# A transformer block pair on one core: seven places for experts' weights and joined 4 MB transfers

## The reference, cut to what matters

```
logits = hf @ w_router + b_router;  top_vals, top_idx = top_k(logits, 4);  top_w = softmax(top_vals)
for every expert e, for the tokens that chose it (xb):
    gu = xb @ w_gate_up[e] + b_gate_up[e]             # 1024 x 2048: gate 1024 columns, up 1024 columns
    g, u = min(gu[:, :1024], 7), clip(gu[:, 1024:], -7, 7)
    y = ((u + 1) * g * sigmoid(1.702 * g)) @ w_down[e] + b_down[e]       # 1024 x 1024
x += the sum over a token's four experts of top_w * y
```

## Time and profile before

| | |
|---|---|
| three runs | 1762.68, 1765.52, 1767.84 us; median 1765.52 |
| span of the profiled execution, first to last instruction | 1762.7 us; its time with what lies around the span isn't recorded apart, the lowest of the three runs is 1762.68 |
| busy, of the span | TensorE 93%, its weight loads 59%, VectorE 40%, ScalarE 32%, GpSimd 1% |
| read from HBM | 544 MB, mean 309 GB/s |
| experts' transfers | 126 + 63 of 2048 KB into the ring, 17.4 and 16.2 us from issue to landing (medians), and a few in pieces |

### The profile page before, as it was taken

The page is one execution under the profiler, slowest core; times in us unless marked ns, Lnnn a source line. Parts: engine busy times, 40 slices in busy tenths (PEclk is TensorE's granted clock), DMA queues, the critical chain, the costliest instruction groups (busy, mean ns, idle before and its releaser), DMA issues.

```text
span 1762.7 us, 20269 instructions
## 1 busy us (share of the span) xinstructions
PE 1643.2 (93%) x8853; PEld 1036.4 (59%) x8854; DVE 707.4 (40%) x876; ACT 571.9 (32%) x787; POOL 22.5 (1%) x37
## 2 busy tenths in 40 slices
PE   8999999898889999998888888999999999999998
PEld 7788533333235454442323232378888998988886
DVE  5897411111121211211111111167664965567663
ACT  6576200011111111100000011175563765456552
POOL 0000000000000000000000000010000000000000
PEclk9999999999999999999999999999999999999999
DMA  7538999999999999999999999955555523445552
GB/s 257 174 103 289 366 392 428 427 428 427 428 427 400 428 427 425 428 427 428 428 428 428 428 427 426 420 189 193 190 192 173 184 96 120 168 132 191 191 191 96
DMA packets 118762, 546.39 MB, mean 310 GB/s; under 512 B 5696, under 2 KB 64192, under 8 KB 92976
## 3 DMA queue, kind: packets, MB, share of 16 engines
q1 hardware_dynamic: 117344, 540.96, 77.4%
q0 software_dynamic: 1040, 4.00, 0.8%
q10 hardware_dynamic: 288, 0.11, 0.0%
HBM read 544.00 MB, written 1.05 MB: 309 GB/s over the span
## 4 chain that ended last, share of the span: by engine, by line
PE 70%; DMA 25%; DVE 3%; ACT 1%; issue 1%; SPq 0%; ACTq 0%
DMA ring<-in_w_down 25%; PE PS L949 10%; PE PS L908 9%; PE PS L578 8%; PE PS L1099 6%; PE PS L580 4%; PE PS L530 2%; PE PS L531 2%; PE PS L532 2%; PE PS L850 2%; PE PS L960 2%; PE PS L563 1%; PE PS L564 1%; PE PS L565 1%; PE PS L1114 1%; PE PS L549 1%
## 5 line engine op out<-in xcount | busy, mean ns | idle before, releaser
L908 PE MATMUL PS<-ring,work 128*64 128x512 f32 x2016 | 448.2, 596 | 36.5 <-DMA ring<-in_w_gate_up 36.4
L1920 DVE TENSOR_TENSOR ring<-ring,ring 128x2048 fp32r<-128x2048 f32 (+2 forms) x130 | 289.3, 2234 | 258.5 <-ACT ring L1341 258.4
L908 PEld LDWEIGHTS PS<-ring,work 128*64 128x64 f32 x2016 | 139.7, 137 | 325.4 <-issue 246.6
L1341 ACT CAST ring<-ring 128x2048 fp32r<-128x2048 f32 (+2 forms) x131 | 242.9, 1866 | 208.8 <-DMA ring<-in_mem_w_kv 86.6
L949 PE MATMUL PS<-ring,work 128*64 128x512 f32 x1024 | 239.1, 611 | 53.8 <-DMA ring<-in_w_down 37.8
L949 PEld LDWEIGHTS PS<-ring,work 128*64 128x64 f32 x1024 | 75.4, 139 | 203.5 <-issue 164.6
L2349 DVE TENSOR_SCALAR work<-PS 128x512 f32<-128x512 f32 x32 | 22.1, 690 | 325.9 <-PE PS L908 325.9
L1596 ACT ACTIVATE work<-work 128x512 f32<-128x512 f32 x32 | 20.2, 630 | 366.2 <-DVE work L2349 366.2
L2248 DVE TENSOR_TENSOR work<-PS,work 128x512 fp32r<-128x512 f32 x32 | 22.1, 692 | 252.2 <-ACT work L1540 252.2
L578 PE MATMUL PS<-xr,ring 128*128 128x512 f32 x320 | 111.2, 392 | 0.0
L578 PE MATMUL PS<-work,ring 128*128 128x512 f32 x320 | 111.2, 392 | 0.0
(11 more groups left out here) (418 smaller groups left out, 2325.1 us busy)
## 6 DMA issues: line engine op xcount, KB each, us to landing
ring<-in_w_gate_up SPq DMA_DIRECT2D x126, 2048.0 KB, 17.4
ring<-in_w_down SPq DMA_DIRECT2D x63, 2048.0 KB, 16.2
ring<-in_ffn_w_gu SPq DMA_DIRECT2D x44, 1024.0 KB, 5.1
ring<-in_w_in SPq DMA_DIRECT2D x28, 1024.0 KB, 5.4
ring<-in_ffn_w_down SPq DMA_DIRECT2D x22, 1024.0 KB, 4.9
ring<-in_w_out SPq DMA_DIRECT2D x8, 1024.0 KB, 5.6
ring<-in_mem_w_kv SPq DMA_DIRECT2D x8, 1024.0 KB, 13.8
ring<-in_w_ple_gate SPq DMA_DIRECT2D x4, 1024.0 KB, 11.6
```

Of the source, the lines that this page charges most:

```text
L908: t = e.matmul(PS[hf * 64:hf * 64 + 64, bank, :], XG[g % 2][:, 2 * kp + kk, i * 64:(i + 1) * 64], raw_chunk(w, kk)[:, c0 + hf * 512:c0 + h ...
L1341: e.copy(hi(j), raw(j)).then_inc(*act.now(("hi", j)))
L1920: e.tensor_tensor(lo(j), raw(j), hi(j).bitcast(F32), ALU.subtract).then_inc(*dve.now(("lo", j)))
```

## The change

The list of parts stays. There are two more places: X, which is the tile `xr` made a sixth place of the ring's tensor (usable once the attention's last product is done, given up at the ple stage), and Y in work space, up to expert `CHECK`, now 6. `place` hands out the place whose part is oldest. Of experts 4 to 29 two neighbouring parts of a matrix go into two neighbouring places by one transfer of 4 MB, if the two oldest places are neighbours; it waits for both. What a partition receives is now the rows of one run of 32 KB, so a single part is half such a run. The two halves of an expert's width are therefore no longer columns 0 to 511 and 512 to 1023: `hidden` takes fours alternately, and the moving operand of gate, up and bias has four floats, then a gap of four. `apart` is issued second. To free the work space, the transposed memory `mT` is spread over leftover places, the masks `C_HM` (512 KB) come in at the end of the memory's products and not at the start, and the normed tokens for the slow path are made only in the slow path.

```diff
-CHECK = 5
+X, Y, APART = NS, NS + 1, NS + 2
+CHECK = 6
+JOINED, FIRST_JOINED = ('w_gate_up', 'w_down'), 4
+    def joined(self, i):
+        p = self.parts[i]
+        if p.name not in JOINED or not FIRST_JOINED <= p.expert < NE - 2:
+            return False
+        return (p.k0 // p.k) % 2 == 0
     def place(self):
+        first, crowded, behind = (self.of[k][0] for k in (("gate_up", 0), ("gate_up", CHECK), ("ple_gate", 0)))
+        count = dict.fromkeys(range(APART + 1), 0)
+        held = {s: s - NS for s in range(NS)}
+        i = 0
+        while i < len(self.parts):
+            if i == first:
+                held[X], held[Y] = self.of["out", 1][1] - 0.5, self.of["out", 1][1] + 0.5
+            if i == crowded:
+                del held[Y]
+            if i == behind:
+                del held[X]
+            oldest = sorted(held, key=held.get)
+            slots = oldest[:1]
+            if i == self.apart:
+                slots = [APART]
+            elif self.joined(i) and max(oldest[:2]) <= X and abs(oldest[0] - oldest[1]) == 1:
+                slots = sorted(oldest[:2])
+            after = [held[s] for s in slots if held.get(s, -1) >= 0]
...
+        early = next(n for n in self.loads if n[0] == self.apart)
+        self.loads.remove(early)
+        self.loads.insert(1 + [n[0] for n in self.loads].index(first), early)
...
+            def hidden(v, hf):
+                return v.rearrange("p (q z r) -> p q z r", z=2, r=4)[:, :, hf, :]
...
-                                             raw_chunk(w, kk)[:, c0 + hf * 512:c0 + hf * 512 + 512], start=False,
+                                             hidden(raw_chunk(w, kk)[:, c0:c0 + DE], hf), start=False,
...
-            e.wait_ge(*dve["factor_out"])
-            for h in range(2):
-                t = e.matmul(RSB[:, h * 128:(h + 1) * 128], rn[:, h:h + 1].to_broadcast([128, 128]), ident, start=True,
-                             stop=True, skip_group_check=True)
-            t.then_inc(*pe.now("rsb"))
...
-            e.dma_start(cst[:, C_HM:C_N], d["cst"][:, C_HM:C_N]).then_inc(hm_in, 16)
...
-                if g == 1:
-                    e.wait_ge(*pe["comb", 0])
+                if g == 5:
+                    e.wait_ge(*pe["beside", MEM_KV[-1]])
                     e.dma_start(p_raw, d["p"].rearrange("(h p) n -> p h n", p=128)).then_inc(p_in, 16)
+                    e.dma_start(cst[:, C_HM:C_N], d["cst"][:, C_HM:C_N]).then_inc(hm_in, 16)
...
+                    for k in after:
+                        e.wait_ge(*pe["w", k if k in plan.slot else of["out", 1][1]])
...
                     if j == plan.apart:
                         e.wait_ge(*pe["merged_t", 3])
-                        e.wait_ge(*act["bias_2", 64])
...
+                    elif n == 2:
+                        s = plan.slot[j]
+                        e.dma_start(ring_t[:, s * SLOT:(s + 2) * SLOT].rearrange("p (k n) -> p k n", n=p.n),
+                                    src).then_inc(in_memory(j)[0], 16)
                     else:
+                        if plan.slot[j] == Y:
+                            e.wait_ge(*pe["logits"])
+                            e.wait_ge(*act["bias_2", 64])
```

More of the change, by code:

```diff
@@ L163, in place @@
[L163 to L169, removed]
+        self.slot, self.at, self.loads = {}, {}, []
@@ new lines, in place @@
+        count = dict.fromkeys(range(APART + 1), 0)
[15 more added lines that the diff above has]
+            after = [held[s] for s in slots if held.get(s, -1) >= 0]
+            count[slots[0]] += 32 if i == self.apart else 16
+            for k, s in enumerate(slots):
+                self.slot[i + k], self.at[i + k] = s, (slots[0], count[slots[0]])
+                if s != APART:
+                    held[s] = i + k
+            self.loads.append((i, len(slots), after))
+            i += len(slots)
@@ L289, in stats, with in_memory @@
             return stat[:, o:o + n]
-        loaded = [sem(f"ring{i}_loaded") for i in range(NS)] + [sem("spare_loaded"), sem("apart_loaded")]
+        loaded = [sem(f"ring{i}_loaded") for i in range(NS)] + [sem(f"{n}_loaded") for n in ("place_x", "place_y", "apart")]
+        def in_memory(i):
+            return loaded[plan.at[i][0]], plan.at[i][1]
         def held(t, i, o):
@@ L1007, in crowded @@
                 with e.If(most > CAP):
+                    for c in range(8):
+                        for h in range(2):
+                            o = PS[:, 4 + c // 2, (c % 2) * 256 + h * 128:(c % 2) * 256 + h * 128 + 128]
+                            for half in (hnh, hnl):
+                                m = e.matmul(o, half[:, h, c * 128:(c + 1) * 128].bitcast(F32), ident, start=half is hnh,
+                                             stop=half is hnl, skip_group_check=True)
+                    m.then_inc(o_turned, 1)
+                    e.wait_ge(o_normed, 1)
                     with e.Fori(0, NE) as n:
@@ L2763, in sync, with load_before @@
             made = [0]
-            def load_to(i):
-                while made[0] <= i:
-                    j, p = made[0], parts[made[0]]
+            def load_before(i):
+                while made[0] < len(plan.loads) and plan.loads[made[0]][0] < i:
+                    j, n, after = plan.loads[made[0]]
                     made[0] += 1
-                    w = d[p.name]
-                    if plan.after[j] is not None:
-                        e.wait_ge(*pe["w", plan.after[j]])
+                    p, w = parts[j], d[parts[j].name]
+                    for k in after:
+                        e.wait_ge(*pe["w", k if k in plan.slot else of["out", 1][1]])
                     if p.name in PACKED:
@@ L2819, in sync @@
                         spilled(n)
-            load_to(len(parts) - 1)
+            load_before(len(parts))
             for h in range(2):
```

73 lines of the change are left out of this document (43 added, 30 removed).

## The result

| | before | after |
|---|---|---|
| median, range | 1766.68 us (1762.68 to 1768.15, 4 runs) | 1789.6 us (1788.03 to 1790.55, 4 runs) |
| ratio, 95% interval | | 1.0135 (1.0121 to 1.0149) |
| span of the profiled execution | 1762.7 us | 1788.7 us |

The forecast said slower, 1772 us with a range to 1785. The sign and the places of the loss were right; the loss of 22.9 us is nearly four times the +6.0 us of the sum, and outside the range.

The account below looks back on a forecast made before the run. The prediction took the DMA engines as the bound from 262 us to the experts' end. From 1765.5 us, -8.8 + 1.2 - 4.6 - 2.8 + 12 + 8.5 + 0.5 = +6.0 gave 1771.5, said as 1772; range 1751 to 1785.

Parts of the forecast that it names:

- The five experts whose pair starves the queue: Second gate/up pair of experts 13, 15, 16, 17, 19: DMA queue idle 2.4 us each, 12 us added.
- The places' gain: Terms for places, masks and the stretch at 524 us: -8.8 + 1.2 - 2.8 us.
- The term of the mem_w_kv stretch: Experts that also load mem_w_kv: 12 us of idle queue and 8.5 us of slower clock, +20.5 us.
- the queue holds 9.8 us: When the down pair lands in the mem_w_kv stretch, one whole pair, 9.8 us of transfer, still stands behind it.
- 2.7 us on top: Same stretch: issue to landing of an idle queue is at least 7.6 us for 4.93 us of bytes.
- The clock's 8.5: First down part before each of the five gaps slowed 1.7 us by a lower TensorE clock, 8.5 us in all.
- About 0.5 us: Crowded check at expert 6: next pair's bytes come at 28.6 us, queue lasts 28.4; bounds 0 to 2.3.
- Two more places: Start of the expert loads, 158 to 262 us: places X and Y and early apart gain 2.8 + 6.0 = 8.8 us.
- A: Rival: the queue starves in the mem_w_kv experts but the clock holds, 1763 us; chance 0.22.
- B: Rival: the queue never starves, loads behind a mem_w_kv part being issued in time, 1750.5 us; chance 0.20.
- C: Rival: the gate/up matmuls' strided moving operand costs a third, 4.6 us per expert, 1797 us; chance 0.07.
- D: Rival: the 4 MB transfer moves its bytes no faster, so no 4.6 us gain, 1776 us; chance 0.13.

Follow-up runs that it names:

- e7: Changed kernel with no joined transfers and the earlier weight layout and gathers, keeping the seven places, early apart and moved masks: 1755.55 us.
- e4: Changed kernel with three pairs of matmuls whose result nothing reads added ahead of the down parts of the mem_w_kv experts: 1786.09 us.
- e5: Changed kernel with the first joined expert 8 instead of 4: 1785.51 us.
- e10: Changed kernel, all pairs kept, with normalised rows written in the gathers' order so their stationary operand is in one piece: 1787.47 us.
- e8: Changed kernel with the mem_w_kv product ahead of the down parts and pairs only for experts 8 to 26: 1754.71 us.
- e1: Changed kernel with every 4 MB transfer taken back to two of 2 MB: 1760.8 us.
- e12: Changed kernel with every 4 MB transfer taken back to two of 2 MB, the same kernel as e1 run again: 1759.4 us.
- e9: The kernel of e8 with normalised rows written in the gathers' order so their stationary operand is in one piece: 1754.72 us.

## Why the prediction was wrong

**Right.** The bound (DMA from 262 us to the end of the experts), and so the rule that idle DMA time moves the end. The five experts whose pair starves the queue, all five. The fall of the clock after gaps of 4 us. The places' gain: e7 gave 1755.55 against 1755.1 from those terms, with some luck, since the trace has 11.7 us at the end of the experts and 10.5 at the end of the span, against 10.4. The hole at 530 closed. The moving operand by fours cost nothing: 32 gate/up matmuls in 7.03 us, 64 in 13.90, as in the earlier trace rows. The rate rose by 0.7% (427 to 428 without pairs, 430 to 431 with them in plain experts; forecast 0.65%).

The Trainium skill (DMA: Bandwidth & Descriptors, Rules for kernel authors) has 1 MiB per transfer for the maximum bandwidth; the trace differs by those 0.7%, and 431 is still short of that page's ceiling of 435.2 GB/s.

**Wrong, in order of size.**

1. The term of the mem_w_kv stretch, +20.5, measured +28.3. The failing step is "the queue holds 9.8 us" at the landing: it held 7.4 to 7.8 in four of the five cases, since TensorE waits for the last of the 16 DMA engines and most of them are 2.0 us into the next transfer by then; in the fifth, where they ended together, it held 9.1. The prediction had folded this with the start-up into "2.7 us on top", against 1.2 + 2.0 = 3.2 us at 658.70. The five holes without the clock are 14.6 us where it had 12, so this step is worth 2.6 us. The clock's 8.5 was right as a sum (8.1), in part by luck: four slow down parts of 1.4 to 2.7 us and not five of 1.7. A sixth hole of 2.1 us, at expert 13's down pair, was not forecast: I followed each hole as if the one before had not happened. It stands in every kernel that has expert 13's first hole (after, e4, e5, e10) and in none without, but that the first makes the second is my reading. The remaining 3.5 us of the lag are in no hole as counted here; that they lie beside the holes, where the rate falls before all engines stop (from 16 busy engines to none between 666.2 and 668.4) and rises again by steps, is likely and not shown.
2. "About 0.5 us" for the crowded check: 4.9. The same early end of most engines (T + 27.6, where the prediction had 28.4), and a chain to the next issue of 30.2 us instead of 26.9, in which only 0.9 us is due to the gathers. The bounds 0 to 2.3 rested on "the 1 us by which a landing trails its bytes".
3. "Two more places" with "6.0 us" from 190 to 262: the lead with the masks was 3.9 instead of 7.6. The working was right for the kernel that it described (e7: 9.2); what it missed is an edit that was in the diff: the gathers' stationary operand. I weighed the loads of every fourth float for the moving operand, with rows in hand, and did not look where the same layout met a stationary one. The comparison was also of unlike loads: the 211 ns are those of transposes, and a transpose's load in one piece took 140 in the same rows; 192 is a matmul's. What is shown is the lead; in time it is worth 0 to 3 us.
4. The last experts, +3.4, forecast 0: most likely the pairs of experts 27 to 29 (e8 leaves them out and loses nothing there). Which wait grows I did not follow.

Points 1 and 2 together are 12.2 us of the 20.0 us between the sum and the profiles, 3 and 4 are 7.1. Two side figures of the prediction don't follow from its own terms and change nothing: with no gain from 4 MB the sum is 1776.1 and not 1776.5, and its 72 pairs at the ceiling that it names would be 8.8 us and not 7.9 below the sum.

**The rivals.** A (the clock holds) is refuted by the rows, and e4 (1786.1 us with the clock up ahead of four of the five holes) shows that it would not have saved the change. B (never starves) needs the place free by T + 7.1; it came at T + 12.2. C is refuted by 13.90 us for 64 gate/up matmuls, D by the rate of 431 GB/s from 800 to 1050 us, where e1 with single parts has 428. The range could have held the result: with every bound on the bad side but the strided operand's 11 us the sum was 1791, and I cut it at 1785.

**Where the change could have gone.** Its three ideas apart: places -10 us (e7). Pairs with the mem_w_kv product in its old position +28.8 (after against e1). Pairs of experts 8 to 26 with the product moved -4.7 and -6.1 (e8 against e12 and e1, on different chips; by the ratios to before on each chip 3.4 and 4.9 us), where 4.6 were forecast for the rate of all pairs; how much of it is the moved product without pairs wasn't tried. The best versions, e8, e9 and e7, are within 1 us of each other, 0.5 to 0.6% below before, so with the gathers of this layout no gain of the pairs over the places alone is shown.

## What to carry to other kernels

Joining transfers into larger ones makes the unit in which places come free larger as well. Before joining, compute for each pair what still stands in the queue when its places come free. Take off what the engines have already moved of the next transfer when the waiting work starts (here about 2 us of 9.8, since that work waits for the last of 16 engines), and move any unrelated work that stands between the uses of its two halves. Do this along the whole sequence with each stall carried forward, since one hole shifts the engine against the queue and can make the next. And when an edit changes a layout, list every reader of that index, stationary and moving, before pricing any.

## What the runs showed of the hardware

- A load of 128 columns of float32 as stationary operand: 188 ns with the floats in one piece (e9), 196 with every second, 330 with every fourth at line 893. In the transposes of the earlier trace rows it is 140 in one piece and 211 with every fourth. So every fourth float adds 142 ns to the one kind and 71 to the other; why isn't shown. As a moving operand four floats on, four off cost nothing (7.03 us for 32 matmuls of 512 columns).
- A run of 32 KB in a partition against two of 16 KB: median 1216 ns in the changed kernel from 800 to 1050 us against 2 x 614 before, and 430 to 431 GB/s against 427 to 428.
- From an issue into an empty queue (670.92) to the first byte 1.0 us, to eight busy engines 1.2 us. From the last byte of a transfer to its last landing 0.5 us, and 0.14 us more to the start of the TensorE work that waits for it (658.70).
- The 16 DMA engines don't end a transfer together: the landings of one 4 MB transfer lie 1.7 us apart at 658.70 and 0.5 us at 623.25, shortly after a stretch in which all engines stood still. The waiting work starts with the last.
- The granted clock fell after partial gaps: 2.18 us ahead of a down pair that then took 8.78 instead of 7.2 us (granted clock 0.80), 2.12 us in e4 and 2.65 us in e10 (5.35 instead of 3.65 us for a down part both times), and not after 2.02 us at 623.25. The earlier trace rows have one fall and one hold after 1.99 and 2.00 us, so the length of the gap alone doesn't decide it.
- The lead at 265 us differed by up to 2.4 us between executions of kernels that are the same up to there, so a difference of 2 us in one profile is no finding by itself.
